# Two DiT-like blocks with compensated fp32r matmuls on one core: the four column groups of a weight chunk take turns in the matmul stream

## What is computed

```python
# first network, layers 0 and 1
h = rmsnorm(x, norm1_g[l]) * (1 + sc1) + sh1
x = x + g1 * token_mix(h, w_in[l], w_fourier[l], w_ret[l], w_out[l])
h = rmsnorm(x, norm2_g[l]) * (1 + sc2) + sh2
x = x + g2 * conv_ffn(h, ffn_up[l], conv_w[l], conv_b[l], ffn_down[l])
# conv_ffn: u = h @ w_up (5632 columns), 3-tap convolution over tokens,
#           (gelu(a) * b) @ w_down
# second network, layers 2 and 3: 256 latent tokens, and 256 context tokens
# that leave after layer 2
h = h + g1 * mix          # pooling, gating and attention branches, merged @ w_o
h = h + g2 * (square(relu(modulated @ w_ff1)) @ w_ff2)
```

## Time and profile before

| | us |
|---|---|
| median of 3 runs | 2298.4 |
| lowest, highest | 2295.4, 2299.55 |
| profiled execution, time (the run that agrees with its span) | 2299.55 |
| profiled execution, span | 2299.5 |
| TensorE busy in it | 2238.4 (97%) |
| VectorE, ScalarE, GpSimd busy | 1518.5, 1006.3, 365.7 |
| mean granted TensorE clock | 0.982 of full speed |

### The profile page before, as it was taken

The page is one execution under the profiler, slowest core; times in us unless marked ns, Lnnn a source line. Parts: engine busy times, 40 slices in busy tenths (PEclk is TensorE's granted clock), DMA queues, the critical chain, the costliest instruction groups (busy, mean ns, idle before and its releaser), DMA issues.

```text
span 2299.5 us, 37596 instructions
## 1 busy us (share of the span) xinstructions
PE 2238.4 (97%) x14564; PEld 2016.0 (88%) x14564; DVE 1518.5 (66%) x2029; ACT 1006.3 (44%) x1491; POOL 365.7 (16%) x262
## 2 busy tenths in 40 slices
PE   7999999999999999999999999999999999999998
PEld 7989999999999999989678777888888787989997
DVE  6655888866657789968555566765555375756554
ACT  3543556635444465443243542432132244665453
POOL 0320203300501113213101002110020120012120
PEclk8999999999999999999799999999999999999999
DMA  8654657676565656652332333344445243644552
GB/s 305 245 187 173 208 196 247 233 253 207 179 220 194 218 175 212 218 212 92 124 119 97 115 115 118 100 156 138 137 155 183 92 146 129 209 149 149 186 183 97
DMA packets 109328, 395.04 MB, mean 172 GB/s; under 512 B 12146, under 2 KB 13810, under 8 KB 108916
## 3 DMA queue, kind: packets, MB, share of 16 engines
q1 hardware_dynamic: 107892, 388.62, 49.2%
q0 software_dynamic: 1280, 4.20, 0.6%
HBM read 391.72 MB, written 1.05 MB: 171 GB/s over the span
## 4 chain that ended last, share of the span: by engine, by line
PE 91%; DVE 6%; issue 1%; DMA 1%; ACT 1%; POOL 0%; SPq 0%; DVEq 0%; ACTq 0%; POOLq 0%
PE bank L512 23%; PE bank L514 23%; PE bank L513 23%; DVE w_lo L1295 2%; PE bank L445 2%; PE bank L568 2%; PE bank L569 1%; PE bank L570 1%; PE bank L814 1%; PE bank L853 1%; DVE acc L1312 1%; PE bank L602 1%; PE bank L660 1%; DMA stage<-in_stream 1%; PE bank L646 1%
## 5 line engine op out<-in xcount | busy, mean ns | idle before, releaser
L1295 DVE TENSOR_TENSOR w_lo<-stage,w_hi 128x1024 fp32r<-128x1024 f32 x536 | 691.1, 1297 | 570.9 <-ACT w_hi L921 569.3
L921 ACT ACTIVATE w_hi<-stage 128x1024 fp32r<-128x1024 f32 x536 | 567.3, 1060 | 966.3 <-PE bank L514 854.7
L512 PE MATMUL bank<-h_hi,w_hi 128*128 128x256 f32 (+1 forms) x2832 | 869.8, 307 | 4.2 <-DVE w_lo L1295 2.6
L513 PE MATMUL bank<-h_lo,w_hi 128*128 128x256 f32 (+1 forms) x2832 | 862.5, 305 | 0.0
L514 PE MATMUL bank<-h_hi,w_lo 128*128 128x256 f32 (+1 forms) x2832 | 862.4, 305 | 0.0
L512 PEld LDWEIGHTS bank<-h_hi,w_hi 128*128 128x128 f32 x2832 | 541.1, 191 | 30.9 <-DVE w_lo L1295 4.6
L513 PEld LDWEIGHTS bank<-h_lo,w_hi 128*128 128x128 f32 x2832 | 541.3, 191 | 23.2 <-issue 0.7
L514 PEld LDWEIGHTS bank<-h_hi,w_lo 128*128 128x128 f32 x2832 | 540.9, 191 | 22.8
L1312 DVE SCALAR_TENSOR_TENSOR acc<-stage,csil,acc 128x512 f32<-128x512 f32 x440 | 368.7, 850 | 24.5 <-DMA stage<-in_stream 1.6
L512 PE MATMUL bank<-f_hi,w_hi 128*128 128x512 f32 (+1 forms) x512 | 174.1, 340 | 0.0
L513 PE MATMUL bank<-f_lo,w_hi 128*128 128x512 f32 (+1 forms) x512 | 173.1, 338 | 0.0
(11 more groups left out here) (212 smaller groups left out, 2892.3 us busy)
## 6 DMA issues: line engine op xcount, KB each, us to landing
stage<-in_stream SPq DMA_DIRECT2D x728, 512.0 KB, 4.0
bias<-in_bias POOLq DMA_DIRECT2D x16, 256.0 KB, 3.1
X<-in_x SPq DMA_DIRECT2D x1, 2048.0 KB, 13.2
decay<-in_decay SPq DMA_DIRECT2D x1, 1024.0 KB, 6.0
out<-X SPq DMA_DIRECT2D x1, 1024.0 KB, 4.8
rope<-in_rope SPq DMA_DIRECT2D x2, 256.0 KB, 3.5
dfts<-in_dfts SPq DMA_DIRECT2D x1, 512.0 KB, 8.3
wsgu<-in_wsgu SPq DMA_DIRECT2D x2, 256.0 KB
```

The lines of the kernel that those rows point to most:

```text
L512: mm(out, w_hi[:, slot, w], xh[:, c, 0:T], start=first, stop=False)
L513: mm(out, w_hi[:, slot, w], xl[:, c, 0:T], start=False, stop=False)
L921: A(w_hi[:, m % NR, :], stage[:, n % NS, :], ACT.Copy).then_inc(hi_ready, 1)
L1295: do(V.tensor_tensor(w_lo[:, m % NR, :], stage[:, n % NS, :], w_hi[:, m % NR, :].bitcast(F32), ALU.subtract), unit_done, done_value(n))
```

## The change

The loop over n moves inside the loop over k and is run three times: four matmuls `w_hi * x_hi`, one in each of the four banks, then four `w_lo * x_hi`, then four `w_hi * x_lo`. The matmuls are the same 24 in a unit; the groups' sums are taken in another order. All four groups are opened by the first four matmuls of the block's first unit, and closed by the last four of its last unit. `units_used`, which frees a weight slot, stays on the last matmul of the unit. Nothing else is touched.

```diff
                     x_ready(i)
-                    for n in range(ng):
-                        if i == 0:
-                            open_group(g0 + n)
-                        out = bank_of(g0 + n)[:, 0:T]
-                        for k in range(KC):
-                            c = k0 + KC * i + k
+                    for k in range(KC):
+                        c = k0 + KC * i + k
+                        first, final = i == 0 and k == 0, i == nu - 1 and k == KC - 1
+                        for n in range(ng):
+                            if first:
+                                open_group(g0 + n)
                             w = slice(k * COLS + n * P, k * COLS + (n + 1) * P)
-                            first, final = i == 0 and k == 0, i == nu - 1 and k == KC - 1
-                            mm(out, w_hi[:, slot, w], xh[:, c, 0:T], start=first, stop=False)
-                            mm(out, w_hi[:, slot, w], xl[:, c, 0:T], start=False, stop=False)
-                            last = mm(out, w_lo[:, slot, w], xh[:, c, 0:T], start=False, stop=final)
-                        if i == nu - 1:
-                            close_group(last, g0 + n)
+                            mm(bank_of(g0 + n)[:, 0:T], w_hi[:, slot, w], xh[:, c, 0:T], start=first, stop=False)
+                        for n in range(ng):
+                            w = slice(k * COLS + n * P, k * COLS + (n + 1) * P)
+                            mm(bank_of(g0 + n)[:, 0:T], w_lo[:, slot, w], xh[:, c, 0:T], start=False, stop=False)
+                        for n in range(ng):
+                            w = slice(k * COLS + n * P, k * COLS + (n + 1) * P)
+                            last = mm(bank_of(g0 + n)[:, 0:T], w_hi[:, slot, w], xl[:, c, 0:T], start=False, stop=final)
+                            if final:
+                                close_group(last, g0 + n)
```

## The result

The changed kernel takes 2337.2 us (median of 3 runs, 2332.0 to 2338.8) against 2298.4: 1.0162 times the time before, 95% interval 1.0147 to 1.0176, 38.8 us more. The forecast was 2312.6 us, slower, with a range up to 2325; the sign was right and the loss was 2.7 times the 14.2 us of the sum. The profiled execution took 2338.84 us, its span is 2337.1.

A forecast was written before the change was run, and what follows sets the result against it. The prediction took TensorE's matmul pace and its few holes to bound the kernel. Stalls of 6.7, 4.4, 0.9, 1.2 and 1.0 us sum to 14.2, giving 2313.7 for the profiled execution and 2312.6 as forecast median; range 2301 to 2325.

The forecast's parts named there:

- The pace: Matmul stream of the changed loop: 0.12 us per 256-column matmul stays, so nothing for 11,856 matmuls.
- The places: TensorE holes after the third matmul: 1.7 us at four layer 0 blocks; 2.2, 1.1 and 1.4 in layer 1.
- (a): Layer 0, up2, up5, up8 and dn0: four stalls of 1.67 us waiting for VectorE's bank, 6.7 us.
- Line 1557's fourth piece follows: Layer 0, dn0 behind up10: VectorE's fourth piece directly follows ScalarE's four reads, 0.05 us hand-over, 0.47 long.
- (b): Layer 1, up5, up10 and dn1: bank waits grow by 1.9, 1.1 and 1.4 us, together 4.4.
- (c): Norm between layers 2 and 3: later reads and square delay TensorE's sums of the last chunk by 0.9 us.
- (d): Last head after ga1 in layer 2: fourth read later, 0.8 us; layer 3 estimated at half; together 1.2.
- (e): Other short covers, rotation behind block k in two layers and layer 3 heads: 1.0 us, bounds 0 and 3.
- Half a read each: Size assumed for the short covers at block k's rotation in two layers and layer 3's heads, together 1.0 us.
- The covers hold: Rival: readers start early enough, no layer 0 stalls, half of two other terms: 3 us, 2301.5; chance 0.12.
- VectorE becomes the bound in layer 1: Rival: later reads cause `w_lo` waits in eleven layer 1 blocks: +5.8 us, 2318, up to 2328; chance 0.17.

The follow-up runs named there:

- the narrowed product: GpSimd's product of the up blocks done on 8 of 256 tokens: in the changed kernel 2316.5 us, in the kernel before 2292.1 us.
- twelve fillers: Changed kernel with 12 extra matmuls between opening the third and fourth group in up2, up5, up8, dn0 of layer 0 and up5 of layer 1: 2331.8 us.
- the run with pairs: Turns over two banks at a time, groups 0 and 1 and then 2 and 3, instead of the changed kernel's four: 2299.0 us, 0.9999 of the kernel before.

## Why the prediction was wrong, point by point

**The pace: right.** No change: 0.120 us a matmul in both traces, and the run with turns between the ends of blocks gives 1.0000.

**The places: right.** Holes stand behind the third matmul of up2, up5, up8 and dn0 in layer 0 and of up5, up10 and dn1 in layer 1, ended by lines 1565 and 1448. With the start of the first unit alone as before, or the end of the last, more than half of the loss goes; with both, all of it.

**(a), the term that failed: 6.7 us forecast, 21.8 measured.** Each seam was put at 1.67 us and costs 5.4 to 5.5. It was mis-sized twice. First, "Line 1557's fourth piece follows" took VectorE to be free, with three pieces behind it, when ScalarE's reads end; no row was given for that. It is not free: line 1560 begins its first piece only at 476.82, after ScalarE's fourth read has ended (476.48), and not piece by piece beside it, because `w_lo` has begun behind GpSimd's operation and takes 2.29 us instead of 1.22. Line 1565 comes 3.91 us behind the last matmul's start, not 2.43; the hole is 3.1 us. Second, the sum priced a hole at its own length. 3.1 us of idling cost another 2.4 at the lower clock, and filling the hole with matmuls of no use gave nearly that back at each place (3.1 to 3.2 us instead of 5.4).

**(b): 4.4 forecast, 9.0 measured** (from 22.2 at the start of up5 to 31.2 at the end of dn1). up10 and dn1 cost 1.6 and 1.5, near the 1.1 and 1.4 forecast. up5, with a hole of 2.6 us and the lower clock behind it, cost 4.8 instead of 1.9, and 1.8 came at the end of up9 from a `w_lo` that was held by GpSimd.

**(c), the norm between layers 2 and 3: 0.9 forecast,** and TensorE's wait for ScalarE's square there is a new 0.9 us. **(d), the last head of layer 2: 0.8 forecast,** as measured in the trace (from ga1's last matmul to ao0's first, 5.8 us before and 6.6 now).

**(d) for layer 3 and (e): mis-sized, 1.4 forecast.** "Half a read each" fits three heads of layer 3 (TensorE waits 0.16 us more) and roughly the last one (0.46), but not the heads behind gp0, which wait 0.73 us in layer 2 and 1.50 in layer 3, where they did not wait before. There ScalarE loads an activation table for 1.28 us before it reads. Of layer 3, before and after:

```profile
1949.78 1.28 ACT L1199 ACT_TABLE_LOAD   x1 [0.53 <-PE bank L514]
```

```profile
1984.99 1.28 ACT L1202 ACT_TABLE_LOAD   x1 [2.33 <-PE bank L517]
```

The load begins when the first group is closed. Before, that was 1.8 us ahead of the start of gp0's last matmul (1951.57), so that the load ran beside the last unit; now it stands behind the last matmul's start (1984.98), and the four reads end 2.5 us behind that start instead of 0.7. And the clock falls behind the wait. Timeline and window of the changed kernel, and the same head before:

```profile
1989.55 3.60 PE L856 MATMUL bank<-pT,v 128*64 128x256 f32 x8 [1.50 <-ACT pT L1178]
```

```profile
1989.50:1993.00 3.50, 3.45 (x8) 1.60 (x8) 2.34 (x6) 3.26 (x7) 0.54 (x1) 0.52 0.54 157
```

```profile
1954.57 1.94 PE L853 MATMUL bank<-pT,v 128*64 128x256 f32 x8
```

Eight matmuls take 3.6 us instead of 1.9: that head alone is 3.2 us, more than all of (d) and (e). From the last matmul of d11 to the end 7.3 us are added; this head and the norm's 0.9 are 4.1 of them, and the rest was not taken apart.

**The rivals.** "The covers hold" did not happen. "VectorE becomes the bound in layer 1" pointed at the right engine and the wrong place: its waits for `w_lo` grew by only 0.8 us in the list. No rival had the clock in it, and the range ended at 2325.

**What was given back** is 3.5 us between layers 1 and 2, most of it the full clock shown above at the first unit of layer 2.

What stays open: why the clock falls behind one hole of 1.1 us and not behind its twin. These twins, the four alike holes with the narrowed product, and the stretches that the changed kernel won without an edit suggest that it depends on when the hole comes. Even executions of one kernel differ: with twelve fillers one took 2321.9 us at a mean clock of 0.985, the others 2331.3 to 2333.3 at 0.978 or 0.979. No run here shifted one hole by a known time, so this is not shown.

## What to carry to other kernels

Before finishing several accumulation groups together, look at who reads them and who waits for their banks: the stagger between groups costs nothing in the matmul stream and was worth 38.8 us here, and turns over two banks keep it. Price a new hole of TensorE as the hole plus the matmuls that may run at the lower clock behind it, 1.4 to 2.4 us here where the clock fell, and nothing where it held. And when a change shifts VectorE by a microsecond, look whether it now starts behind a GpSimd operation where it had started ahead of it.

## What the hardware showed that was not expected

- Two holes alike in every engine's busy time (TensorE idle for 0.92 us) left different clocks. Behind idle stretches of 2.9 us the clock fell at all four places of layer 0. Behind 1.4 to 1.5 us it held at all four with twelve fillers, and at two of four with the narrowed product.
- Matmuls of no use in a wait shortened what follows: each place of layer 0 cost 3.1 to 3.2 us instead of 5.4, though the wait ended no sooner.
- A `w_lo` that starts under a GpSimd operation is mostly held until that one ends (49 of 63 in the kernel before; 2.29 instead of 1.22 us in the rows above), and a GpSimd subtraction that starts under a `w_lo` is held likewise (2.29 us at 386.27 of the run with pairs, 1.46 at 351.74 of the changed kernel, where only the end of an operation of VectorE lay over it). The mean over the 536 `w_lo` is 1297 ns before, 1334 after, and 1299 with both ends as before. A mean that moves by 3% hides single operations that double, at the one place where a bank is waited for.
